# Expert retrieval in blocks: the query projection cut by heads and placed among the gathers, routes read from PSUM

## The chip, the cores and the metric

One core of a Trainium2 chip runs the whole kernel. The metric is the device time of one execution in microseconds, the median of three runs.
## The reference

One layer of a hybrid decoder, for a prompt of 512 tokens and eight samples of eight tokens (576 tokens in all, width 1024). The first half mixes tokens (an mLSTM branch and dilated window attention, merged by gates and projected); it also returns the caches rolled on by eight tokens. The second half, with which the change deals, is a product-key expert retrieval:

```
def _peer(h, wq, k1, k2, u, v):                       # h: (576, 1024), 8 heads, top 16
    q = (hb @ wq).reshape(blk, P_HEADS, P_QDIM)       # 8 heads x 256
    s1 = jnp.einsum('thd,nd->thn', q[..., :P_HALF], k1)
    s2 = jnp.einsum('thd,nd->thn', q[..., P_HALF:], k2)
    v1, i1 = lax.top_k(s1, P_TOPK)
    v2, i2 = lax.top_k(s2, P_TOPK)
    cand = v1[..., :, None] + v2[..., None, :]        # 16 x 16 candidates per head
    sc, pos = lax.top_k(cand, P_TOPK)
    eidx = take(i1 * P_NKEYS + i2, pos)               # 16 of 16384 experts
    g = jax.nn.softmax(sc, axis=-1)
    act = jax.nn.gelu(einsum('td,thkd->thk', hb, u[eidx]))
    return einsum('thk,thkd->td', g * act, v[eidx])
```

The result is normalised, scaled by a modulation row and added to the residual. Each token and head fetches 16 rows of u and v, 8 KB together.

## The kernel before

Tokens lie in five tiles: tiles 0 to 3 are the prompt (128 tokens each), tile 4 holds the 64 sample tokens. The program is a row of blocks with a barrier between them, each engine with its own instruction stream in the order in which the code is written; semaphores tie the streams together. Copies of the caches from memory to memory ("rolls", 88 pieces of up to 1 MB, `roll_pieces`) are issued by POOL beside the stages: one per unit of a projection (L399), two per step of the prompt attention (L599), one per unit of the merge gates (L731). SyncE waits for all of them at the very end (L1606).

`output_projection` (L1394) produces x1, h2 (tokens on partitions) and, by transposes, h2T (channels on partitions); beside it SyncE loads the first two of four 2 MB query weights. `query_projections` (L1509, through `project`, L372) multiplies all of h2T by all query weights: 16 units of 128 features, each of 8 matmuls of 288 columns for either half of the tokens, taken by ScalarE into qT. During it neither VectorE nor the gathers run.

`peer` (L1543) is the expert stage. Its unit is a slot n: one expert of one head for the 128 tokens of a tile. For each tile and head there is a *route* on VectorE (L1721 to L1759): two top-16 searches over 128 scores, 256 candidates, a top 16 of them, expert indices and softmax weights. ScalarE copies the scores of a whole tile out of PSUM first (`scores_taken`, L1665). For each slot POOL issues an indirect DMA of 128 rows of 8 KB, 1 MB (L1622), into one of `RING` = 10 slots; VectorE takes the dot product with h2 (L1767); ScalarE forms gelu, coefficient and a diagonal matrix (L1690, L1694, L1698), two slots at a time (`BATCH`); TensorE adds diagonal times v row in PSUM by two matmuls, four records (L1652), and so frees the slot, for which POOL waits:

```
if n >= RING:
    pool.wait_ge(s_v, n - RING + 1)
```

The order is tile by tile, head by head: 8 heads of tiles 0 to 3, and for tile 4 four pairs of heads packed into 128 partitions (POOL's copy, L1612), 36 blocks of 16 slots, 576 slots. `routed_beside` and `routed_at` (L1520, L1529) place the routes: beside tile 0 two per head (its own next one and tile 1's), beside tiles 1 and 2 one, beside tile 3 one for half of the heads, beside tile 4 none. At a tile's start TensorE computes the scores of the next tile (16 products, L1633), and at slot 4 the tile before is finished: ScalarE squares, VectorE mean, ScalarE root, VectorE scale and residual (`finish`).

## Time and profile before

| what | value |
|---|---|
| median of three runs | 2789.01 us (2787.6 to 2793.09) |
| profiled execution, its own time | 2792.53 us |
| its span, first to last instruction | 2790.7 us |
| mean granted TensorE clock | 0.904 |
| busy: PE, DVE, ACT, POOL | 2255.7, 1245.6, 703.4, 689.0 us |
| bytes moved by DMA | 850.42 MB, 691.32 of them on POOL's queue |

The profile is one execution, as the hardware recorded it. A group of instructions stands under its line in the code, with what it writes and reads, its count and its mean duration; behind it stands how long the engine had been idle just before and who ended that wait. Busy time of TensorE counts overlapping records once. "DMA share" is the mean busy share of the sixteen DMA engines; values up to 1.02 occur by rounding of the records. Idle time of an engine costs nothing where another sets the pace.

### The profile page before, as it was taken

How to read it: one execution, taken by the hardware profiler on the slowest of the kernel's cores; microseconds unless marked ns; L12 is line 12 of the kernel's file. 1: busy time of each engine (PE TensorE's matmuls, PEld its weight loads, DVE VectorE, ACT ScalarE, POOL GpSimd, SP SyncE). 2: the span in 40 equal slices, each digit the busy share in tenths (PEclk: the TensorE clock that was granted, in tenths of full speed). 3: DMA queues.
4: the chain of work that ended last, by engine and by line, in shares of the span. 5: the costliest groups of instructions: out<-in, count | busy, mean ns of one | idle time of the engine just before them, and what ended most of it. 6: DMA issues, size and time to landing. Idle time of an engine off the chain costs nothing.

```text
span 2790.7 us, 25027 instructions
## 1 busy us (share of the span) xinstructions
PE 2255.7 (81%) x9058; PEld 1285.6 (46%) x9058; DVE 1245.6 (45%) x3220; ACT 703.4 (25%) x2110; POOL 689.0 (25%) x682
## 2 busy tenths in 40 slices
PE   7999989966699978896777778777777877777776
PEld 2777458855478854475333333323332332332221
DVE  1000001211044422203899866776677677654544
ACT  2100012310023111101343333333333333322222
POOL 0000000000010000001443444444444444444342
PEclk8999989977789889998898898899888988999999
DMA  7666446879552025012999999999999999999997
GB/s 283 235 270 266 169 165 226 300 321 365 213 210 75 26 91 188 8 61 108 405 419 418 413 417 394 420 419 417 398 421 419 420 418 400 420 420 420 421 419 310
DMA packets 128002, 850.42 MB, mean 305 GB/s; under 512 B 14865, under 2 KB 24369, under 8 KB 46589
## 3 DMA queue, kind: packets, MB, share of 16 engines
q0 software_dynamic: 85760, 691.32, 60.8%
q1 hardware_dynamic: 40828, 154.95, 14.7%
q10 hardware_dynamic: 1290, 2.55, 0.3%
q8 instruction: 71, 1.16, 0.2%
q14 instruction: 53, 0.43, 0.0%
HBM read 836.43 MB, written 99.37 MB: 335 GB/s over the span
## 4 chain that ended last, share of the span: by engine, by line
DMA 20%; DVE 15%; PE 13%; ACT 2%; issue 2%; POOL 1%; ACTq 0%; POOLq 0%
DMA pr_ring<-in_uv,pr_idx 20%; PE ps L1652 12%; DVE pr_ring L1767 5%; POOL pr_ring L1622 1%; DVE pr_hot L1750 1%; DVE pr_hot L1746 1%; ACT pr_coef L1694 1%; DVE pr_ind L1725 1%; DVE pr_ind L1722 1%; DVE pr_pick L1753 1%; DVE pr_val L1724 1%; DVE pr_rest L1723 1%; DVE pr_val L1721 1%; DVE pr_pos L1725 1%; ACT pr_diag L1698 1%
## 5 line engine op out<-in xcount | busy, mean ns | idle before, releaser
L1652 PE MATMUL ps<-pr_ring,pr_diag 128*128 128x512 f32 (+1 forms) x2304 | 1097.8, 634 | 373.3 <-ACT pr_diag L1698 373.1
L1652 PEld LDWEIGHTS ps<-pr_ring,pr_diag 128*128 128x128 f32 (+1 forms) x2304 | 443.6, 198 | 1024.6 <-issue 517.2
L1767 DVE CUSTOM_DVE_ANT_0 pr_ring<-pr_ring,h 128x1024 f32<-128x1024 f32 x576 | 688.7, 1224 | 398.3 <-DMA pr_ring<-in_uv,pr_idx 396.9
L1622 POOL DMA_INDIRECT pr_ring<-in_uv,pr_idx x576 | 634.5, 1102 | 833.6 <-PE ps L1652 784.5
L1690 ACT ACTIVATE pr_gel<-pr_dots 128x2 f32<-128x2 f32 x288 | 58.6, 204 | 814.5 <-DVE pr_dots L1767 814.5
L1698 ACT ACTIVATE pr_diag<-ident,pr_coef 128x128 f32<-128x128 f32 x512 | 173.5, 386 | 0.0
L399 POOL DMA_DIRECT2D out_win_s<-in_cache x40 | 19.7, 492 | 569.4 <-PE ps L431 468.7
L1694 ACT ACTIVATE pr_coef<-pr_gel,pr_wgt 128x1 f32<-128x1 f32 x576 | 138.6, 287 | 27.1 <-ACT pr_gel L1690 0.4
L714 PE MATMUL ps<-trunk,gate_ring 128*128 128x288 f32 x512 | 130.3, 416 | 0.0
L430 PE MATMUL ps<-trunk,ap_ring 128*128 128x288 f32 x384 | 126.5, 411 | 2.9 <-PEq L323 2.9
L431 PE MATMUL ps<-trunk,ap_ring 128*128 128x288 f32 x384 | 125.7, 410 | 0.0
L1273 PE MATMUL ps<-sa_ring,sa_spread 128*32 128x128 f32 x1664 | 78.7, 371 | 51.3 <-DMA sa_ring<-in_cache 25.2
L299 DVE TENSOR_TENSOR late_rows<-ps,late_bias 128x512 f32<-128x512 f32 x2 | 1.4, 692 | 252.8 <-PE ps L289 252.8
L714 PEld LDWEIGHTS ps<-trunk,gate_ring 128*128 128x128 f32 x512 | 99.0, 195 | 27.2 <-ACT gate L722 0.3
L434 PE MATMUL ps<-ap_ring,trunk 128*128 128x512 f32 (+1 forms) x240 | 104.5, 595 | 0.0
L643 DVE CUSTOM_DVE_ANT_0 pa_prob<-ps,pa_masks 128x256 f32<-128x256 f32 (+3 forms) x48 | 19.4, 455 | 186.4 <-PE ps L608 186.4
L1273 PEld LDWEIGHTS ps<-sa_ring,sa_spread 128*32 128x32 f32 x1664 | 70.9, 152 | 60.0 <-issue 59.0
L1721 DVE MAX8 pr_val<-pr_sc 128x8 f32<-128x128 f32 x72 | 21.1, 293 | 152.5 <-ACT pr_sc L1665 151.2
L430 PE MATMUL ps<-h2T,qp_ring 128*128 128x288 f32 x256 | 84.3, 411 | 1.1 <-PEq L1412 1.1
L430 PEld LDWEIGHTS ps<-trunk,ap_ring 128*128 128x128 f32 x384 | 73.3, 192 | 23.8 <-issue 4.2
L431 PE MATMUL ps<-h2T,qp_ring 128*128 128x288 f32 x256 | 83.7, 409 | 0.0
L431 PEld LDWEIGHTS ps<-trunk,ap_ring 128*128 128x128 f32 x384 | 73.7, 192 | 20.4
(297 smaller groups left out, 2170.7 us busy)
## 6 DMA issues: line engine op xcount, KB each, us to landing
out_win_s<-in_cache POOLq DMA_DIRECT2D x64, 1020.0 KB, 7.1
late_ring<-in_w_ada SPq DMA_DIRECT2D x8, 2048.0 KB, 17.7
sa_ring<-in_kcacheB SPq DMA_DIRECT2D x8, 2048.0 KB, 12.8
sa_ring<-in_cache SPq DMA_DIRECT2D x8, 2048.0 KB, 13.8
out_win_s<-in_cache POOLq DMA_DIRECT2D x16, 1008.0 KB, 6.0
ap_ring<-in_w_attn_qk SPq DMA_DIRECT2D x6, 2048.0 KB, 11.2
sa_ring<-in_kcacheA SPq DMA_DIRECT2D x8, 1280.0 KB, 13.8
pr_ring<-in_uv,pr_idx POOLq DMA_INDIRECT x576, 14.6
```

The source lines that it names most:

```text
L430: pe.matmul(ps[:, u % 2, 0:TH], wc, rhsT[:, c, 0:TH], **on)
L431: mm = pe.matmul(ps[:, 2 + u % 2, 0:TH], wc, rhsT[:, c, TH:T], **on)
L434: mm = pe.matmul(ps[0:r, u % 2, :], rhsT[:, c, tile_cols(j)], w[:, c, :], **on)
L714: mm = pe.matmul(self.k.ps[:, self.BANK + half, 0:TH], self.ring[:, u % self.AHEAD, c, :], self.k.hT[:, c, half * TH:(half + 1) * TH], sta ...
L1273: mm = pe.matmul(o, operand(n // 2, s, w), ring[:, n % SR, (u * H + h) * P:(u * H + h + 1) * P], start=False, stop=last, skip_group_check= ...
L1622: pool.indirect_dma_start(ring[:, n % RING, :], None, d["uv"], bass.IndirectOffsetOnAxis(ap=idx[:, i % 2, q:q + 1], axis=0)).then_inc(arri ...
L1652: mm = pe.matmul(ps[0:r, 4 + 2 * (i % 2) + half, :], diag[:, n % RING, 0:r], ring[:, n % RING, o:o + CHUNK], start=q == 0, stop=q == last)
L1690: act.activation(gel[:, o:o + BATCH], dots[:, o:o + BATCH], ACT.Gelu).then_inc(s_gel, 1)
L1694: act.activation(coef[:, o + b:o + b + 1], gel[:, o + b:o + b + 1], ACT.Copy, scale=wgt[:, i % 2, q + b:q + b + 1]).then_inc(s_cf, 1)
L1698: act.activation(diag[:, o + b, 0:r], k.ident[:] if i < PT else k.fold[:], ACT.Copy, scale=coef[:, o + b:o + b + 1]).then_inc(s_dg, 1)
L1725: return dve.max_index(index[0:r, 8:16], out[0:r, 8:16], rest_)
L1767: ins = dve.tensor_tensor_reduce(u, u, e.h2[:, i, :], 1.0, 0.0, ALU.mult, ALU.add, dots[:, n % RING:n % RING + 1])
```

## The change

The block of the query projections is gone. Its work is cut into 32 pieces of 8 matmuls: for each head two halves of 128 features for the 384 tokens of tiles 0 to 2 (pieces 0 and 1) and two for the 192 tokens of tiles 3 and 4 (pieces 2 and 3). Head 0's pieces stand at the start of `peer`; those of head h + 1 stand in the blocks of head h (`query_pieces`): pieces 0 and 1 behind the first and the fifth pair of slots of tile 0's block, piece 2 behind the fifth pair of tile 1's, piece 3 behind the first of tile 2's. ScalarE takes each two pairs later. There is one PSUM bank for queries, one for scores and six for the sums of three tiles.

The slots now go head by head through tiles 0 to 2 (24 blocks), then through tile 3 and tile 4 (12 blocks). Scores are computed for one block, two blocks ahead; VectorE searches them where they lie in PSUM, and the copies to SBUF and POOL's packing are dropped. A route stands in every block ahead of its seventh pair of slots, for the block two further on. Finishing a tile is spread over four steps. Query weights are loaded per head, 1 MB in rows of 1 KB, two ahead of the stage and six within it. h2T lies in the half of `trunk` that the output projection does not read. The prompt attention issues three rolls per step.

```diff
                 for s in range(N):
                     pool.wait_ge(s_t, s + 1)
-                    for _ in range(min(2, len(k.rolls))):
+                    for _ in range(min(3, len(k.rolls))):
...
-                for n in range(e.wq.slots):
-                    sp.dma_start(e.wq.w[:, n], d["peer_wq"][n]).then_inc(e.wq.ready[n], 16)
-                e.wq.loaded = e.wq.slots
+                for h in range(QUERY_SLOTS):
+                    load_query_weights(sp, d, e, h)
...
+GROUP = 3
+GROUPED = GROUP * P
+BLOCKS = [(i, h) for h in range(PH) for i in range(GROUP)] + [(i, h) for i in range(GROUP, NCH) for h in range(heads_of(i))]
+FINAL = {i: b for b, (i, _) in enumerate(BLOCKS)}
+QUERY_SLOTS = 2
+QUERY_BANK, SCORE_BANK, SUM_BANK = 0, 1, 2
+def query_pieces(i, h, q):
+    return [piece for piece, at in enumerate(((0, 0), (0, 4), (1, 4), (2, 0))) if at == (i, q) and h + 1 < PH]
+def load_query_weights(sp, d, e, h):
+    o = h % 2 * 2 * P
+    sp.dma_start(e.wq[:, h % QUERY_SLOTS], d["peer_wq"][h // 2][:, :, o:o + 2 * P]).then_inc(e.wq_ready[h % QUERY_SLOTS], 16)
 RING = 10
-FINISH = 4
 BATCH = 2
+PER = TOPK // BATCH
+ROUTE, SCORE = 6, 2
+SQUARE, MEAN, ROOT, FINISH = 2, 3, 4, 5
...
+        def query_of(i, f):
+            if i < GROUP:
+                return first[:, f % 4, tile_cols(i)]
+            o = (i - GROUP) * P
+            return e.later[:, f, o:o + tile_rows(i)]
...
+                for h in range(QUERY_SLOTS, PH):
+                    sp.wait_ge(s_q, 4 * (h - QUERY_SLOTS + 1))
+                    load_query_weights(sp, d, e, h)
...
+                for b in range(len(BLOCKS)):
+                    pool.wait_ge(s_idx, b + 1)
+                    for j in range(TOPK):
+                        n = b * TOPK + j
                         if n >= RING:
                             pool.wait_ge(s_v, n - RING + 1)
                         pool.indirect_dma_start(ring[:, n % RING, :], None, d["uv"],
-                                                bass.IndirectOffsetOnAxis(ap=idx[:, i % 2, q:q + 1], axis=0)
+                                                bass.IndirectOffsetOnAxis(ap=idx[:, b % 4, j:j + 1], axis=0)
...
+                def query(h, piece):
+                    group, half = divmod(piece, 2)
+                    cols = slice(GROUPED, T) if group else slice(0, GROUPED)
+                    if piece == 0:
+                        pe.wait_ge(e.wq_ready[h % QUERY_SLOTS], 16 * (h // QUERY_SLOTS + 1))
+                    pe.wait_ge(s_qt, 4 * h + piece)
+                    for c in range(KD):
+                        mm = pe.matmul(ps[:, QUERY_BANK, 0:cols.stop - cols.start],
+                                       e.wq[:, h % QUERY_SLOTS, c, half * P:(half + 1) * P], e.h2T[:, c, cols],
+                                       start=c == 0, stop=c == KD - 1)
+                    mm.then_inc(s_q, 1)
+                def scores(b):
+                    i, h = BLOCKS[b]
+                    r = tile_rows(i)
+                    pe.wait_ge(s_qt, 4 * h + (2 if i < GROUP else 4))
+                    if b >= 1:
+                        pe.wait_ge(s_idx, b)
+                    for half in range(2):
+                        for o, head in ((0, h),) if i < PT else ((0, h), (TS, h + PH // 2)):
+                            mm = pe.matmul(ps[o:o + r, SCORE_BANK, half * P:(half + 1) * P], query_of(i, 2 * head + half),
+                                           keysT[:, half, :], start=True, stop=True)
                     mm.then_inc(s_sc, 1)
+                query(0, 0)
+                query(0, 1)
                 pe.wait_ge(s_keys, 16)
                 scores(0)
...
+                scores(1)
+                query(0, 2)
+                query(0, 3)
+                for b, (i, h) in enumerate(BLOCKS):
+                    r, bank = tile_rows(i), SUM_BANK + 2 * (i % GROUP)
+                    if i >= GROUP and h == 0:
+                        pe.wait_ge(s_ft, i - GROUP + 1)
+                    for q in range(PER):
+                        for j in range(q * BATCH, (q + 1) * BATCH):
+                            n = b * TOPK + j
+                            pe.wait_ge(s_dg, n + 1)
+                            for half in range(2):
+                                o = D + half * CHUNK
+                                mm = pe.matmul(ps[0:r, bank + half, :], diag[:, n % RING, 0:r],
+                                               ring[:, n % RING, o:o + CHUNK], start=h == 0 and j == 0,
+                                               stop=b == FINAL[i] and j == TOPK - 1)
+                            mm.then_inc(s_v, 1)
+                        if q == SCORE and b + 2 < len(BLOCKS):
+                            scores(b + 2)
+                        for piece in query_pieces(i, h, q):
+                            query(h + 1, piece)
...
+                def query_taken(h, piece):
+                    group, half = divmod(piece, 2)
+                    f = 2 * h + half
+                    act.wait_ge(s_q, 4 * h + piece + 1)
+                    if group == 0:
+                        ins = act.activation(first[:, f % 4, :], ps[:, QUERY_BANK, 0:GROUPED], ACT.Copy)
+                    else:
+                        ins = act.activation(e.later[:, f, :], ps[:, QUERY_BANK, 0:T - GROUPED], ACT.Copy)
+                    ins.then_inc(s_qt, 1)
...
+                query_taken(0, 0)
+                query_taken(0, 1)
+                route_exp(0)
+                query_taken(0, 2)
+                query_taken(0, 3)
+                for b, (i, h) in enumerate(BLOCKS):
+                    for q in range(PER):
+                        if b == 0 and q == 1:
+                            route_exp(1)
+                        if q == ROUTE and b + 2 < len(BLOCKS):
+                            route_exp(b + 2)
+                        if b >= 1 and FINAL[BLOCKS[b - 1][0]] == b - 1:
+                            if q == SQUARE:
+                                square(BLOCKS[b - 1][0])
+                            if q == ROOT:
+                                root(BLOCKS[b - 1][0])
+                        for piece in query_pieces(i, h, q - 2):
+                            query_taken(h + 1, piece)
+                        diags(b, q)
+                square(NCH - 1)
+                root(NCH - 1)
...
+                def route(b):
+                    dve.wait_ge(s_sc, b + 1)
+                    if b >= 4:
+                        dve.wait_ge(s_v, (b - 3) * TOPK)
                     for half in range(2):
-                        chain.step(top16(r, sc[:, i % 2, 2 * h + half, :], rest[:], val[:, half, :], ind[:, half, :]))
+                        chain.step(top16(ps[:, SCORE_BANK, half * P:(half + 1) * P], rest[:], val[:, half, :], ind[:, half, :]))
...
+                route(0)
                 dve.wait_ge(s_in, 16 * (2 + NS))
-                for i in order:
-                    for h in range(heads_of(i)):
-                        for q in range(h * TOPK, (h + 1) * TOPK, BATCH):
-                            if i and q == FINISH:
-                                finish(i - 1)
-                            for t, g in routed_at(i, q):
-                                route(t, g)
-                            dots_of(i, q)
+                for b in range(len(BLOCKS)):
+                    for q in range(PER):
+                        if b == 0 and q == 1:
+                            route(1)
+                        if q == ROUTE and b + 2 < len(BLOCKS):
+                            route(b + 2)
+                        if b >= 1 and FINAL[BLOCKS[b - 1][0]] == b - 1:
+                            if q == MEAN:
+                                mean(BLOCKS[b - 1][0])
+                            if q == FINISH:
+                                finish(BLOCKS[b - 1][0])
+                        dots_of(b, q)
+                mean(NCH - 1)
...
-        e.x1, e.h2, e.qT = sb("x1", [P, NCH, D]), sb("h2", [P, NCH, D]), trunk
-        with ExitStack() as mid:
-            e.h2T = sb("h2T", [P, KD, T], F32, mid)
-            e.wq = weight_ring(nc, k, "qp", mid, 2)
-            output_projection(nc, k, d, e)
-            query_projections(nc, k, d, e)
+        e.x1, e.h2, e.h2T = sb("x1", [P, NCH, D]), sb("h2", [P, NCH, D]), trunk[:, KD:, :]
+        e.wq = sb("pr_wq", [P, QUERY_SLOTS, KD, 2 * P])
+        e.wq_ready = [k.sem(f"pr_wq_ready{r}") for r in range(QUERY_SLOTS)]
+        free = trunk[:, 0:KD, :].rearrange("p c t -> p (c t)")
+        e.first = free[:, 0:4 * GROUPED].rearrange("p (f t) -> p f t", f=4)
+        e.later = free[:, 4 * GROUPED:].rearrange("p (f t) -> p f t", f=2 * PH)
+        output_projection(nc, k, d, e)
```

TensorE's stream from the last query matmuls into the expert stage, before the change (qp_ring and pr_wq are the query weights, trunk holds queries or h2T, pr_keysT the keys, pr_ring the gathered rows; a matmul counts once here):

```order
L431 MATMUL ps<-h2T,qp_ring 128x288
L391 UNCONDITIONAL_BRANCH
L1626 UNCONDITIONAL_BRANCH
L1633 MATMUL ps<-pr_keysT,trunk 128x128 x32
L1652 MATMUL ps<-pr_ring,pr_diag 128x512 x256
L1633 MATMUL ps<-pr_keysT,trunk 128x128 x16
L1652 MATMUL ps<-pr_ring,pr_diag 128x512 x256
```

The same place with the change:

```order
L1619 UNCONDITIONAL_BRANCH
L1629 MATMUL ps<-trunk,pr_wq 128x384 x16
L1642 MATMUL ps<-pr_keysT,trunk 128x128 x4
L1629 MATMUL ps<-trunk,pr_wq 128x192 x16
L1663 MATMUL ps<-pr_ring,pr_diag 128x512 x4
L1629 MATMUL ps<-trunk,pr_wq 128x384 x8
L1663 MATMUL ps<-pr_ring,pr_diag 128x512 x8
L1642 MATMUL ps<-pr_keysT,trunk 128x128 x2
L1663 MATMUL ps<-pr_ring,pr_diag 128x512 x8
L1629 MATMUL ps<-trunk,pr_wq 128x384 x8
L1663 MATMUL ps<-pr_ring,pr_diag 128x512 x24
```

Of 256 query matmuls (the first row stands for the last of them) 16, of 384 columns, are left ahead of the first scores; 16 of 192 columns follow, and the next head's stand between the sums.

POOL's stream in the prompt attention:

```order
 L599 DMA out_win_s<-in_cache 16x16320 x25
-L599 DMA out_win_s<-in_cache 16x16128 x7
+L599 DMA out_win_s<-in_cache 16x16128 x16
+L599 DMA out_win_s<-in_cache 16x7680 x7
 L584 UNCONDITIONAL_BRANCH
```

Sixteen rolls more are issued there, 7 of them half-size.

## Rows read from the trace of the kernel before

**Rows 1.** The page, in 40 slices of the span: GB/s moved by DMA.
```profile
GB/s 283 235 270 266 169 165 226 300 321 365 213 210 75 26 91 188 8 61 108 405 419 418 413 417 394 420 419 417 398 421 419 420 418 400 420 420 420 421 419 310
```
**Rows 2.** Busy us by stretch: PE, PEld, DVE, ACT, POOL, PEclk, DMA share, GB/s.
```profile
1161.00:1288.00 127.00, 125.90 (x512) 98.40 (x512) 0.00 (x0) 11.27 (x33) 0.49 (x1) 0.99 0.10 37
1288.00:1308.00 20.00, 9.28 (x64) 8.92 (x64) 9.35 (x39) 3.88 (x8) 1.24 (x3) 0.83 0.19 59
1400.00:1600.00 200.00, 156.45 (x311) 66.20 (x310) 179.77 (x520) 78.74 (x239) 83.65 (x78) 0.86 1.01 417
1700.00:1960.00 260.00, 191.41 (x405) 80.44 (x404) 184.45 (x469) 84.38 (x278) 113.89 (x102) 0.88 1.01 419
2480.00:2740.00 260.00, 190.93 (x414) 65.11 (x415) 129.72 (x212) 66.66 (x264) 103.70 (x104) 0.99 1.01 420
```
**Rows 3.** Timeline, 1160 to 1308 us: start, duration, instruction, [idle before, releaser].
```profile
1160.41 0.60 ACT L1476 ACTIVATE h2T<-ps 128x512 f32<-128x512 f32 x1 [3.96 <-PE ps L1448]
1161.49 1.30 PE L430 MATMUL ps<-h2T,qp_ring 128*128 128x288 f32 x2 [1.11 <-PEq L1412]
...
1290.33 5.47 PE L1633 MATMUL ps<-pr_keysT,trunk 128*128 128x128 f32 x32 [2.94 <-DMA pr_keysT<-in_keysT]
...
1297.93 0.30 DVE L1721 MAX8 pr_val<-pr_sc 128x8 f32<-128x128 f32 x1 [138.72 <-ACT pr_sc L1665]
...
1307.41 0.23 DVE L1759 TENSOR_SCALAR pr_wgt<-pr_ex,pr_rex 128x16 f32<-128x16 f32 x1
...
1307.93 1.02 POOL L1622 DMA_INDIRECT pr_ring<-in_uv,pr_idx  x1 [18.35 <-DVE pr_wgt L1759]
```
**Rows 4.** The chain of waits, last two of its transfers: start, us until landed.
```profile
2731.74 18.66 DMA pr_ring<-in_uv,pr_idx
2756.68 18.64 DMA pr_ring<-in_uv,pr_idx
```
**Rows 5.** Tile pr_ring, issue to landing: all 576 gathers, then those of 1400:1640.
```profile
DMA to landing us min/median/max: 5.7/14.6/19.9
...
DMA to landing us min/median/max: 8.6/12.1/19.2
```
**Rows 6.** Tile h2T: ns min/median/max, first and last start in us.
```profile
L431 PE MATMUL ps<-h2T,qp_ring x256: 405/407/688, 1162.6 to 1287.0; 128*128 128x288 f32 x128
```
**Rows 7.** DMA queues in 391:516 (rolls on q0, mp_ring on q1): packets, MB, share.
```profile
q0 software_dynamic: 656, 21.94, 47.9%
q1 hardware_dynamic: 5200, 5.24, 13.3%
```
**Rows 8.** Timeline of PE: a run of 512-column records; the first behind a route.
```profile
1104.72 13.90 PE L1438 MATMUL ps<-op_w,trunk 128*128 128x512 f32 x32
...
1388.70 0.70 PE L1652 MATMUL ps<-pr_ring,pr_diag 128*128 128x512 f32 x1 [3.56 <-ACT pr_diag L1698]
```
**Rows 9.** Groups of DVE: one operand in PSUM, then all in SBUF.
```profile
L1117 DVE TENSOR_TENSOR ml_hn<-ml_iw,ps 128x512 f32<-128x512 f32 (+1 forms) x5 | 3.4, 683 | 0.3 <-ACT ml_iw L1070 0.3
L1120 DVE TENSOR_TENSOR ml_hn<-ml_hn,ml_rd 128x512 f32<-128x512 f32 (+1 forms) x5 | 3.4, 689 | 0.2
```
**Rows 10.** Busy us by stretch, the end of tile 0 (columns of Rows 2).
```profile
1670.00:1690.00 20.00, 11.75 (x22) 5.16 (x23) 17.15 (x38) 8.02 (x28) 4.49 (x5) 0.67 0.85 342
```
**Rows 11.** Prompt attention's end and sample attention: stretches, POOL's last rolls.
```profile
520.00:550.00 30.00, 30.00 (x163) 24.36 (x162) 8.77 (x30) 16.44 (x26) 2.89 (x6) 1.00 0.99 379
550.00:583.00 33.00, 27.27 (x160) 22.88 (x158) 3.01 (x10) 9.65 (x19) 1.93 (x4) 0.97 0.53 189
583.00:660.00 77.00, 45.22 (x896) 38.92 (x896) 10.26 (x32) 1.28 (x1) 0.00 (x0) 0.68 0.99 408
...
571.53 0.96 POOL L599 DMA_DIRECT2D out_win_s<-in_cache  x2 [9.27 <-PE ps L622]
```
**Rows 12.** Timeline of the output projection's first tile.
```profile
1095.87 0.16 DVE L1487 TENSOR_TENSOR op_ss<-op_ss 128x1 f32<-128x1 f32 x1 [33.26 <-DMA op_rows<-rows]
...
1103.79 1.09 PE L1448 MATMUL ps<-ident,h 128*128 128x128 f32 x8 [2.72 <-DVE h L1506]
```

204 lines of the change are left out of this document (63 added, 141 removed).

## The prediction, made before the run

> **What bounds the kernel now.** I read the page's slices first, then the busy time by stretch, then the chain of waits and the transfers' landing times. The slices show one stage that fills half the program [rows 1]: from slice 20 on the DMA engines are full and move about 420 GB/s, while the three slices before the ramp (1116 to 1325 us) move 8, 61 and 108 GB/s. The stretches name both sides [rows 2]. From 1161 to 1288 us the query projections keep TensorE busy for 125.90 of 127 us while the DMA share is 0.10; from 1288 to 1308 us scores and the first route run, at 0.19. Then the gathers run: DMA share 1.01 wherever one looks, VectorE at 90%, 71% or 50% busy, TensorE at 74 to 78%. So the expert stage is bound by bytes: 576 gathers of 1.05 MB. The first is issued at 1307.93 [rows 3], the last at 2756.68 [rows 4], 575 intervals in 1448.8 us, 2.52 us each. Where no route is computed the chain repeats every ten gathers in 24.94 us [rows 4], 2.49 each, the pure price of the bytes.
>
> Two things follow. The time before the first gather is wholly on the path and holds little DMA work; and work put beside the gathers is free as long as the ring of ten slots never empties. The landing times measure that reserve: the first gather, alone, lands 5.7 us after its issue; with two routes per sixteen gathers (tile 0) the shortest is 8.6, the median 12.1 [rows 5], still at share 1.01. At its tightest the ring has 8.6 - 5.7 = 2.9 us to spare.
>
> **The change, part by part.** All sums are against the profiled run: span 2790.7, its own time 2792.5. The median of the runs is 2789.0, 3.5 below, and the sum is carried over to it.
>
> *Start of the gathers.* Of the stretch from 1161.49 to 1307.93 (146.4 us) only two query pieces, one pair of score products and one route stay ahead of the first gather. The projection rows [rows 6] put a 288-column record at (1287.0 - 1162.6) / 255 / 2 = 0.244 us, so 384 columns are 0.325 and a piece of 8 matmuls (16 records) 5.2 us. The query bank is single, so the second piece waits for ScalarE's copy: about 0.9 us, estimated from 0.60 for a 512-wide copy [rows 3] and two handovers, once for each piece. The first records run at the lower clock (1.30 us for two [rows 3]): 1 us. Scores are 4 records of some 0.17 (32 take 5.47 [rows 3]), 0.7 with the drain. The route takes 9.7 us (1297.93 to 1307.64) and POOL issues 0.3 later [rows 3]. Sum 1 + 5.2 + 0.9 + 5.2 + 0.9 + 0.7 + 0.2 + 10.0 = 24.1, plus 0.9 of allowance for further handovers: first gather at 1186.5, **-121.4**. If both pieces ran wholly at the lower clock it would be -111; without the allowance -122.3. The copies of scores by ScalarE and POOL's packing lie in the same stretch and go with it. Group 1's first two pieces stand behind the first gather, in time that TensorE spends waiting for dots.
>
> *Weights beside the gathers.* Six of the eight 1 MB head weights now load in a stage that is full. Their rows are 1 KB runs, like the loads of mp_ring, which stand alone on q1 in [rows 7]: 5.24 MB in 5200 packets for 13.3% of 125 us = 16.6 us of all engines. Six loads are 6.29 MB: **+19.9**. At the gathers' own 420 GB/s it would be 15.0, the lower bound; twice the measured price, 40, is the upper, should two queues disturb each other. The Trainium skill (DMA: Bandwidth & Descriptors, Specifications) gives 512 B as the smallest transfer at line rate; by it these loads would cost the 15.0. The row of 1 KB packets gives 315 GB/s and so disagrees, and I go by the row.
>
> *Query pieces on TensorE.* In tile 0 TensorE is busy 156.45 of 200 us [rows 2], 31.3 per 40 us block of sixteen gathers, against 27.8 (64 records at 13.90 / 32 = 0.434 [rows 8]) at full clock; the rest is the slower clock after each route, behind which it stands idle 3.56 us [rows 8]. A block of tile 0 gets two pieces of 5.2 us: 41.7 against the 39.9 that its bytes take. Blocks of tiles 1 and 2 get one 192-column piece of 2.6 us and stay at 34. So seven blocks are over by 1.8 us, 13 us in all if the ring carries nothing; the next block has 6 us in hand to recover. The first piece stands six gathers behind the end of a route; by then TensorE, at 1.74 us a gather, has gained 6 x (2.49 - 1.74) = 4.5 us on the DMA, with the 2.9 of reserve 7.4, above 5.2. I take **+4** (0 to 13). ScalarE copies a piece before the pair two steps on, with TensorE still holding one pair (3.5 us) against the copy and the pair's own 1.7 us: no stall. Each block now has one route where tile 0 had two; VectorE has time (184.45 busy of 260 with one [rows 2]).
>
> *Route from PSUM.* The same instructions read the score bank. An add out of PSUM took 683 ns, the same form out of SBUF 689 [rows 9]: nothing. Maxima are not shown from PSUM; at 0.1 us more for each of the 6 reads, or less, a route changes by 0.6 us, under VectorE's 11 us of slack per block: 0. Were VectorE full, it would be 36 x 0.6 = 22.
>
> *Tile ends.* Where a tile ends, sixteen score products, the copy, the finish and routes come together, and the DMA runs short: in the worst of four such windows 342 GB/s [rows 10] against 420, 3.7 us; the others are 2.3 to 3.3, some 12 us in all. Scores come by the block now and the finish is split over four steps, but VectorE still waits for the last product of the finished tile. Half goes: **-6** (0 to -12).
>
> *Rolls.* Sixteen cache copies leave the later stages for the prompt attention, three per step; seven are half-size, and these come last. From 520 to 550 us that stage is already at share 0.99 [rows 11]; the three extra copies there take 3 x 2.7 us of all engines (rolls cost 47.9% x 125 / 21.94 = 2.7 us a megabyte [rows 7]), a backlog of 8 us. Behind it there is room (share 0.53 to 583), and the last two steps, one of them at 571.53, now carry 1.5 MB in place of 2. So nothing should reach the sample attention, which is at 0.99 from 583 on [rows 11] and would feel it: **0** (0 to 3). The stages they leave are TensorE's: 0.
>
> *Output projection.* VectorE starts on op_rows at 1095.87 and TensorE then waits 2.72 us for it [rows 12]; the weight loads queued behind are halved: **-1** (0 to -2.7).
>
> Sum: -121.4 + 19.9 + 4 + 0 - 6 + 0 - 1 = -104.5; the span becomes 2686.2, the run's own time 2688.0, and from the median 2789.0 - 104.5 = **2684.5 us**. The tail behind the last gather keeps its form.
>
> **The rivals.** (a) *The ring runs dry at the pieces.* For it: 41.7 against 39.9, and ScalarE is now tied to TensorE at four points per head. Against: the reserve of 7.4 us. If every block of tile 0 loses between its whole excess and one piece, 7 x 1.8 = 13 to 7 x 5.2 = 36 us in place of the 4: 2693 to 2717. (b) *The loads are dear.* Weights at 40 instead of 19.9, rolls at 3: 2708. (c) *The other side: no piece is hidden.* If at each of the 28 pieces the DMA stood still for the piece's length, 7 x (2 x 5.2 + 2 x 2.6) = 109 us come back in place of the 4; with the boundary gain gone too, 2684.5 + 105 + 6 = 2795, slower. It decides from (104.5 - 6 + 4) / 28 = 3.7 us lost per piece. Against it is the 1.01 share with landings down to 8.6 us [rows 2, 5]. It would come about if TensorE's granted clock, 0.86 with two routes per block and 0.99 with none [rows 2], stayed near the lower level (1.2 GHz) while pieces are added; but the clock is lowest here where TensorE idles behind routes [rows 8], and those become fewer in tile 0, so I give the case little. The Trainium skill (TensorE: Matmul & The Clock Gate, Part 1) says that activity releases the clock and idling withdraws it; by that rule the pieces would raise the granted clock, and the time would stay that of the forecast. (d) *The start does not move* because something else holds the first gather. The weights of head 0 are issued in the stage before, and keys and gates land while the pieces run; I see nothing.
>
> **How the numbers follow.** Forecast 0.75 (its own range 2668 to 2704: from -4.9 for the weights, -4, -6 and -1.7 below to 9 for the pieces, 6 for the tile ends, 3 and 1 above); (a) 0.12; (b) 0.07; (c) 0.05; (d) 0.01. The range runs from 2668 to 2720, into (a) and (b). Within 0.2% (5.6 us, about what a measurement of this kernel can tell from no change) needs a near cancellation: 0.01. Faster 0.94, slower 0.05.
>
> **What would show it.** The first gather at about 1186 us and the last about 1469 us behind it: (1448.8 + 19.9 + 4 - 6). DMA share 1.00 or more in the blocks of tiles 0 to 2; the shortest landing there not under 6 us; TensorE near 90% busy in tile 0's blocks. A gather interval above 2.58 us in the first 24 blocks with DMA share under 0.97 would show (a); full share with fewer gathers per us, (b). A sample attention that starts or ends late would show the rolls. The prediction is wrong if the first gather is later than 1200, or if VectorE's reads of PSUM lengthen a route beyond 11 us.

## The result, and the profile after

| | before | after |
|---|---|---|
| median of the runs, us | 2788.31 (2787.44 to 2793.09, 4 runs) | 2682.59 (2675.73 to 2688.66, 4 runs) |
| ratio | | 0.9617, 95% interval 0.959 to 0.9643 |
| profiled run, its own time and span | 2792.53, 2790.7 | 2688.66, 2686.9 |
| first gather, last gather | 1307.93, 2756.68 | 1186.09, 2652.93 |
| between the two | 1448.75 | 1466.84 |

The change takes 105.7 us off the median; 104.5 were forecast. From profile to profile it is 2792.53 - 2688.66 = 103.9. The runs of after lie 12.9 us apart, so an agreement to 1 us is closer than the forecast could be by its own working, and is in part luck. The profiled run of after is the slowest of its four, so terms of a few us are read inside the expert stage and not from these times.

The page of after: busy times, the slices, and the two large DMA queues.

```profile
PE 2238.8 (83%) x9074; PEld 1277.5 (48%) x9074; DVE 1248.4 (46%) x3220; ACT 695.9 (26%) x2094; POOL 702.0 (26%) x680
...
PEclk8999989986798969979899998999898898998889
DMA  6666648989821021339999999999999999999997
GB/s 271 227 256 262 224 169 291 336 339 384 320 84 68 20 95 72 93 140 418 416 418 413 416 416 406 417 411 419 406 420 412 416 420 411 416 411 410 413 420 303
...
q0 software_dynamic: 85760, 691.32, 63.5%
q1 hardware_dynamic: 48572, 154.95, 15.4%
```

Against [rows 1] the full slices begin at 1209 us instead of 1325 (the nineteenth slice of 67.2 us, the twentieth of 69.8), and they read 406 to 420 GB/s throughout.

The timeline of after, from the end of the output projection to the first gather (start, duration, instruction, [idle before, releaser]):

```profile
1160.29 8.37 PE L1629 MATMUL ps<-trunk,pr_wq 128*128 128x384 f32 x16 [1.26 <-PEq L1412]
...
1169.23 5.43 PE L1629 MATMUL ps<-trunk,pr_wq 128*128 128x384 f32 x16 [0.58 <-ACT trunk L1681]
...
1175.33 0.68 PE L1642 MATMUL ps<-pr_keysT,trunk 128*128 128x128 f32 x4 [0.67 <-ACT trunk L1681]
1176.05 0.30 DVE L1750 MAX8 pr_val<-ps 128x8 f32<-128x128 f32 x1 [18.19 <-PE ps L1642]
...
1185.57 0.23 DVE L1785 TENSOR_SCALAR pr_wgt<-pr_ex,pr_rex 128x16 f32<-128x16 f32 x1
...
1186.09 1.07 POOL L1615 DMA_INDIRECT pr_ring<-in_uv,pr_idx  x1 [354.78 <-DVE pr_wgt L1785]
```

From the first query product to the first gather it is 25.8 us where [rows 3] has 146.4: two pieces, two copies, one pair of scores, one route. The first piece takes 8.37 us and the same work right behind it 5.43; the granted clock of the stretch is 0.76, the first row below. The other three rows are the expert stage in stretches, with the columns of [rows 2].

```profile
1160.00:1186.00 26.00, 14.53 (x37) 7.96 (x37) 9.09 (x38) 2.66 (x5) 0.00 (x0) 0.76 0.14 45
1200.00:1860.00 660.00, 562.43 (x1422) 269.38 (x1421) 454.93 (x1135) 215.00 (x716) 287.37 (x252) 0.92 1.01 415
1860.00:2160.00 300.00, 246.40 (x603) 114.90 (x604) 210.54 (x515) 104.75 (x349) 137.59 (x120) 0.91 1.01 414
2160.00:2640.00 480.00, 363.00 (x817) 143.37 (x816) 334.30 (x811) 160.16 (x531) 208.60 (x190) 0.89 1.01 415
```

The DMA share is full in all three stretches of the stage, and TensorE has room: 562.43 of 660 us in the busiest. The stage is bound by bytes as before, starts 121.8 us earlier and lasts 18.1 longer. Below are the times from a gather's issue to its landing, of all 576 and then of those issued in 1200 to 1850. The shortest are close to those of [rows 5], the median of all is the same, and that of the busy blocks is 14.2 where tile 0 had 12.1 before.

```profile
DMA to landing us min/median/max: 5.5/14.6/21.5
```
```profile
DMA to landing us min/median/max: 8.6/14.2/21.4
```

### The profile page after: what moved, and what is told of

It reads as the page before. It is cut to its first block, busy times and chain, and to the rows that moved or that the text cites. A ratio compares the mean times of both kernels' runs of the same rounds, so it can differ in the third digit from the quotient of the medians.

```text
span 2686.9 us, 25099 instructions
## 1 busy us (share of the span) xinstructions
PE 2238.8 (83%) x9074; PEld 1277.5 (48%) x9074; DVE 1248.4 (46%) x3220; ACT 695.9 (26%) x2094; POOL 702.0 (26%) x680
## 4 chain that ended last, share of the span: by engine, by line
DMA 18%; DVE 17%; PE 16%; issue 2%; ACT 2%; POOL 1%; ACTq 0%; POOLq 0%
DMA pr_ring<-in_uv,pr_idx 18%; PE ps L1663 16%; DVE pr_ring L1793 4%; POOL pr_ring L1615 1%; DVE pr_hot L1773 1%; DVE pr_hot L1777 1%; DVE pr_ind L1754 1%; DVE pr_ind L1751 1%; DVE pr_pick L1780 1%; ACT pr_coef L1715 1%; DVE pr_val L1753 1%; DVE pr_rest L1752 1%; DVE pr_val L1750 1%; DVE pr_pos L1754 1%; DVE pr_pos L1751 1%
## 5 line engine op out<-in xcount | busy, mean ns | idle before, releaser
L1615 POOL DMA_INDIRECT pr_ring<-in_uv,pr_idx x576 | 649.1, 1127 | 1173.5 <-PE ps L1663 782.9
L1629 PE MATMUL ps<-trunk,pr_wq 128*128 128x192 f32 (+1 forms) x512 | 134.3, 417 | 2.3 <-PEq L1412 1.3
L1629 PEld LDWEIGHTS ps<-trunk,pr_wq 128*128 128x128 f32 x512 | 93.9, 196 | 48.1 <-issue 17.8
L434 PE MATMUL ps<-ap_ring,trunk 128*128 128x512 f32 (+1 forms) x240 | 104.5, 595 | 0.0
L1437 PE MATMUL ps<-op_w,trunk 128*128 128x512 f32 (+1 forms) x160 | 71.8, 609 | 10.7 <-DMA op_w<-in_w_out 10.7
## 6 DMA issues: line engine op xcount, KB each, us to landing
late_ring<-in_w_ada SPq DMA_DIRECT2D x8, 2048.0 KB, 17.5
pr_ring<-in_uv,pr_idx POOLq DMA_INDIRECT x576, 14.6
```

Source lines behind the costliest of these rows:

```text
L434: mm = pe.matmul(ps[0:r, u % 2, :], rhsT[:, c, tile_cols(j)], w[:, c, :], **on)
L1437: mm = pe.matmul(ps[0:r, 2 * (i % 2) + n, :], k.hT[:, c, tile_cols(i)], w[:, n, c, :], start=c == 0, stop=c == KD - 1)
L1615: pool.indirect_dma_start(ring[:, n % RING, :], None, d["uv"], bass.IndirectOffsetOnAxis(ap=idx[:, b % 4, j:j + 1], axis=0)).then_inc(arri ...
L1629: mm = pe.matmul(ps[:, QUERY_BANK, 0:cols.stop - cols.start], e.wq[:, h % QUERY_SLOTS, c, half * P:(half + 1) * P], e.h2T[:, c, cols], sta ...
```

## The experiments

Each edit is made in the changed kernel. "Stage" is the time from the first to the last gather, "start" that from the first query product to the first gather, both from the profile. The measure for what a profile can tell of the stage: after has 1466.84, and `rolls_two`, whose stage is the same code, 1464.55. So a difference under some 2.4 us is none; three further kernels whose edits barely touch the stage, `first_tile_first`, `scores_copied` and `finish_together`, lie between 1464.46 and 1465.66. The start is 24.3 to 25.9 us in the nine profiles that have this code.

**Query pieces ahead of the stage.**

```diff
-                    for c in range(KD):
+                    for c in range(KD if h == 0 else 1):
...
+                for h in range(1, PH):
+                    for w in (GROUPED, GROUPED, T - GROUPED, T - GROUPED):
+                        for c in range(KD):
+                            pe.matmul(ps[:, QUERY_BANK, 0:w], e.wq[:, 0, c, 0:P], e.h2T[:, c, 0:w], ...)
                 pe.wait_ge(s_keys, 16)
                 scores(0)
```

> The seven later heads' query pieces inside the expert stage shrink to one product of eight each, and TensorE does the same amount of products (112 of 384 columns, 112 of 192) before the first scores; the queries of heads 1 to 7 are therefore partial sums. Theory (the start of the gathers is on the path one for one, pieces beside them are nearly free): first gather later by 14 x 5.2 + 14 x 2.6 = 109 us, at about 1295; first to last gather 1463 to 1467; time about 2682.6 + 109 - 4 = 2788. Rival (work ahead of the stage is partly regained inside it, because something else sets the stage's length): less than 90 us longer. Rival (pieces beside the gathers cost their own length): first to last gather shrinks by 60 to 100 us and the time stays near 2700.

Measured: 2790.47 us (2787.37 to 2795.06, 10 runs), ratio to before 1.0008 (0.9998 to 1.0018). The timeline:

```profile
1151.57 7.74 PE L1629 MATMUL ps<-trunk,pr_wq 128*128 128x384 f32 x16 [1.26 <-PEq L1412]
...
1159.89 5.43 PE L1629 MATMUL ps<-trunk,pr_wq 128*128 128x384 f32 x16 [0.58 <-ACT trunk L1687]
...
1165.89 108.91 PE L1652 MATMUL ps<-trunk,pr_wq 128*128 128x384 f32 x448 [0.58 <-ACT trunk L1687]
...
1285.31 1.07 POOL L1615 DMA_INDIRECT pr_ring<-in_uv,pr_idx  x1 [459.08 <-DVE pr_wgt L1791]
```

108.91 us of products stand ahead of the scores, and the time grows by 2790.47 - 2682.59 = 107.9. The stage is 1466.32 us. The time before the first gather counts one for one, within a few us, and this alone takes back the whole gain.

**Pieces inside the stage, shrunk to an eighth.** The first line of the diff above alone.

> Only the reduction of the pieces inside the stage (one product of eight; the queries of heads 1 to 7 are partial sums), nothing added ahead. It measures what the pieces cost where they are. Theory: 4 us less, between 0 and 13: 2679, first to last gather 1463. Rival (ring runs dry at the pieces): 13 to 36 less. Rival (pieces are not hidden): about 95 less.

Measured: 2679.31 us (2676.7 to 2683.75), 0.961 (0.9594 to 0.9626). The stage is 1466.0 us, no shorter than the changed kernel's beyond what profiles differ by. So seven eighths of the twenty-eight pieces' work cost nothing that shows beside the gathers; the rivals of 13 to 36 and of 95 us fall.

**Pieces inside the stage, issued twice.**

```diff
-                    for c in range(KD):
+                    for c in list(range(KD)) * (1 if h == 0 else 2):
```

> Every product of the pieces inside the stage for heads 1 to 7 is issued twice (the queries come out doubled). A tile-0 block of TensorE goes from 41.7 to 52.1 us, blocks of tiles 1 and 2 from 34 to about 37, against 39.9 of bytes: a group of three blocks is 126 against 120. Theory (only what goes over the bytes' time is paid, and it is recovered little): tile-0 blocks lengthen by some 7 to 12 us each, 50 to 85 us in all, time 2735 to 2765. Rival (the ring and the roomy blocks behind carry most of it): under 30 us, below 2712. Rival (every added us is paid): 109 us, 2790.

(The second round starts its sum anew, so the queries are computed twice and not doubled.) Measured: 2719.32 us (2714.34 to 2720.79), 0.975 (0.9734 to 0.9766): 36.7 us over the changed kernel, below the theory's 50 to 85 and above the rival's 30. The stage is 1498.12 us, 31.3 longer. Stretches of the length of three blocks, one each of tiles 0, 1 and 2 (a group): the changed kernel, the same with light pieces, and the same with double ones. In the first and the last the stretch begins within 2 us of a block of tile 0, in the light one 11 us behind it.

```profile
1303.00:1429.00 126.00, 106.82 (x271) 50.95 (x270) 86.30 (x212) 40.75 (x137) 54.51 (x48) 0.92 1.01 415
```
```profile
1303.00:1429.00 126.00, 95.48 (x212) 41.59 (x212) 87.10 (x217) 41.52 (x137) 53.92 (x48) 0.87 1.01 418
```
```profile
1303.00:1349.00 46.00, 41.79 (x106) 20.07 (x105) 31.28 (x81) 13.37 (x45) 18.43 (x18) 0.96 1.00 408
1349.00:1384.00 35.00, 35.00 (x93) 17.18 (x93) 20.70 (x43) 10.51 (x39) 14.06 (x14) 1.00 0.91 370
...
1303.00:1429.00 126.00, 117.91 (x332) 61.15 (x331) 82.67 (x198) 37.53 (x130) 51.78 (x48) 0.97 0.98 401
```

Here is the limit that the prediction's rival (a) describes: with TensorE busy for all of 35 us the DMA share falls to 0.91 and 370 GB/s. The change itself stays short of it over this group, at 1.01 and 415 GB/s, against 418 with light pieces. The second thing to see is the granted clock: 0.87 with light pieces, 0.92 with the change's, 0.97 with double ones. In these three kernels it rises with the work.

**No weight loads in the stage.**

```diff
-                for h in range(QUERY_SLOTS, PH):
-                    sp.wait_ge(s_q, 4 * (h - QUERY_SLOTS + 1))
-                    load_query_weights(sp, d, e, h)
...
-                        pe.wait_ge(e.wq_ready[h % QUERY_SLOTS], 16 * (h // QUERY_SLOTS + 1))
+                        pe.wait_ge(e.wq_ready[h % QUERY_SLOTS], 16)
```

> The six head weights are not loaded inside the stage; heads 2 to 7 multiply by the weights of heads 0 and 1 again (their queries are those heads'). Theory: six loads cost 3.1 us of all transfer engines each, so the first to last gather shrinks by 19 us and the time is 2664. Rival (the loads cost the gathers' own price per byte): 15 less, 2668. Rival (two queues disturb each other): 25 to 40 less. Rival (transfers are not what bounds the stage in the blocks with pieces): under 10 less.

Measured: 2666.25 us (2663.06 to 2668.61), 0.9554 (0.9538 to 0.957). The stage is 1447.74 us, 19.1 shorter than after and 16.8 shorter than that of `rolls_two`; the time is 16.3 shorter. These lie between the theory's 19 and the 15 of the rival (the gathers' own price per byte) and do not part the two; the next run does. The rivals of 25 to 40 and of under 10 fall. Without the loads the stage is as long as before the change (1448.75): within the 2.4 us that profiles differ by, they are the whole of the 18.1 us by which it grew.

**Weights in long rows.**

```diff
-    sp.dma_start(e.wq[:, h % QUERY_SLOTS], d["peer_wq"][h // 2][:, :, o:o + 2 * P])...
+    sp.dma_start(e.wq[:, h % QUERY_SLOTS], d["peer_wq"][h])...
...
-        "peer_wq": chunks(a["peer_wq"][0]),
+        "peer_wq": np.stack([by_row(a["peer_wq"][0][:, o:o + 2 * P]) for o in range(0, PH * 2 * P, 2 * P)]),
```

> The same 1 MB head weights, but laid out so that each partition's part of one head is a single run of 8 KB and not eight runs of 1 KB. Theory (1 KB runs move at 315 GB/s of all engines, 8 KB runs at 420): six loads cost 15.0 instead of 18.7 to 19.9, so 4 to 5 us less, about 2678; the queue's transfer time in the stage falls from 3.1 to 2.5 us a load. Rival (the run length does not matter): no difference, q1's time unchanged.

Measured: 2678.43 us (2672.98 to 2681.42), 0.9598 (0.9585 to 0.9611), stage 1460.85. DMA queues and issues in 1200 to 1800 us (packets, MB, share of 16 engines), of the changed kernel and then of this one:

```profile
q1 hardware_dynamic: 5341, 5.39, 2.6%
...
pr_wq<-in_peer_wq SPq DMA_DIRECT2D x5, 1024.0 KB, 26.6
```
```profile
q1 hardware_dynamic: 773, 5.55, 2.2%
...
pr_wq<-in_peer_wq SPq DMA_DIRECT2D x5, 1024.0 KB, 9.2
```

2.6% of 600 us for 5.39 MB are 2.89 us a megabyte; 2.2% for 5.55 MB are 2.38. On 6.29 MB that is 18.2 against 15.0, 3.2 us less; the stage shrank by 6.0 against after and 3.7 against `rolls_two`, the time by 4.2. The intervals of the two times overlap, so it is the queue's own rows that settle it (the shares are rounded to 0.1, which leaves each price open by some 0.05). A load also lands in 9.2 us instead of 26.6.

**Tile 0's columns first.**

```diff
+                def first_tile():
+                    pe.wait_ge(e.wq_ready[0], 16)
+                    for half in range(2):
+                        for c in range(KD):
+                            mm = pe.matmul(ps[:, 6 + half, 0:P], e.wq[:, 0, c, half * P:(half + 1) * P],
+                                           e.h2T[:, c, 0:P], start=c == 0, stop=c == KD - 1)
+                    mm.then_inc(s_f1, 1)
...
-                query(0, 0)
-                query(0, 1)
+                first_tile()
                 pe.wait_ge(s_keys, 16)
                 scores(0)
+                query(0, 0)
+                query(0, 1)
```

> Ahead of the first gather only tile 0's 128 columns of head 0 are projected (into the sum banks of tile 2, one copy), the other columns of tiles 1 and 2 follow behind the first scores. Theory (the path to the first gather counts one for one): 32 records of about 0.11 to 0.2 us and one copy in place of two pieces of 8.4 and 5.4 and two copies, first gather at 1177 to 1179 in place of 1186.1, time 7 to 9 us less, about 2675. Rival (the stage's first gathers then wait for scores of tile 1 that come too late): first gather earlier, but the second block's gathers later, no gain.

Measured: 2672.52 us (2670.05 to 2675.51), 0.9585 (0.9572 to 0.9598), 10.1 less than the changed kernel. Its timeline:

```profile
1151.28 5.89 PE L1626 MATMUL ps<-trunk,pr_wq 128*128 128x128 f32 x32 [1.11 <-PEq L1412]
...
1157.20 0.38 ACT L1736 ACTIVATE trunk<-ps 128x256 f32<-128x256 f32 x1 [6.40 <-PE ps L1626]
1157.73 0.68 PE L1653 MATMUL ps<-pr_keysT,trunk 128*128 128x128 f32 x4 [0.56 <-ACT trunk L1736]
...
1168.95 1.07 POOL L1616 DMA_INDIRECT pr_ring<-in_uv,pr_idx  x1 [343.38 <-DVE pr_wgt L1800]
```

The start falls from 25.8 to 17.7 us and the stage stays (1465.26). The pieces that follow cover the other 256 columns. Again one for one as far as it can be read: 8 us of the 10 are in the start, and the other 2 are within what the stages before it vary by (below).

**Fewer copies in the prompt attention.**

```diff
-                    for _ in range(min(3, len(k.rolls))):
+                    for _ in range(min(3 if s == 0 else 2, len(k.rolls))):
```

> Two cache copies per step of the prompt attention as before the change (three in its first step, since one place behind is gone); fifteen copies go back beside the convolution, gates and mLSTM. Theory: no difference (0 to 3 us), sample attention starts within 1 us of before. Rival (the change's 1.4 us of earlier sample attention came of the copies): sample attention later by 1.4. Rival (the copies held something up): 3 us and more less.

Measured: 2683.21 us (2682.11 to 2683.77), 0.9621 (0.9607 to 0.9636). Sample attention starts at 581.75, in after at 581.76, and at 583.32 before the change. In the eleven other profiles it starts between 581.4 and 583.6, `pieces_double` last, so the start before the change is inside the spread. The moved copies cost and gained nothing that shows.

**Scores copied to SBUF.**

```diff
+                def copy_scores(b):
+                    act.wait_ge(s_sc, b + 1)
+                    act.activation(score[:], ps[:, SCORE_BANK, 0:2 * NKEYS], ACT.Copy).then_inc(s_cp, 1)
...
-                    dve.wait_ge(s_sc, b + 1)
+                    dve.wait_ge(s_cp, b + 1)
```

> ScalarE copies the scores of each block to SBUF and VectorE's maxima read the copy, as before the change, in the new block order. Theory: reading the scores from PSUM costs VectorE nothing, the copy of 256 columns stands only in front of the first gather: plus 0.5 to 1 us in all, time the same; a route is as long as before. Rival (maxima are slower from PSUM): a route shortens by over 0.5 us and the stage with it. Rival (ScalarE is tight): the stage gets longer by 5 us and more.

Measured: 2681.98 us (2678.74 to 2683.06), 0.9614 (0.9599 to 0.9629); stage 1464.46. VectorE's groups of the changed kernel, reading PSUM, and of this one, reading the copy:

```profile
L1750 DVE MAX8 pr_val<-ps 128x8 f32<-128x128 f32 x72 | 21.4, 297 | 19.4 <-PE ps L1642 18.2
...
L1751 DVE FIND_INDEX8 pr_ind<-pr_val,ps 128x8 uint32<-128x128 f32 x72 | 20.9, 291 | 0.0
```
```profile
L1760 DVE MAX8 pr_val<-pr_score 128x8 f32<-128x128 f32 x72 | 21.1, 292 | 19.9 <-ACT pr_score L1694 18.6
L1761 DVE FIND_INDEX8 pr_ind<-pr_val,pr_score 128x8 uint32<-128x128 f32 x72 | 20.5, 285 | 0.0
```

Out of PSUM the two take 5 and 6 ns longer, hundredths of a microsecond in a route of 9.8. Leaving the copy out gains nothing that shows in the stage; ahead of the first gather it is 0.4 us (start 26.2 for 25.8).

**The tile's finish in one step.**

```diff
-SQUARE, MEAN, ROOT, FINISH = 2, 3, 4, 5
+SQUARE, MEAN, ROOT, FINISH = 2, 2, 2, 2
```

> Square, mean, root and finish of a tile stand at one step (the third pair of the next block) again, instead of in four steps. Theory (part of the 6 us forecast for the tile ends comes from spreading them): 3 to 6 us longer over the four tile ends inside the stage, mostly in blocks 22 to 24 and 32. Rival (they come by the new order and the scores by the block alone): under 1.5 us.

Measured: 2682.07 us (2676.63 to 2683.75), 0.9613 (0.9595 to 0.9632); stage 1465.66. The blocks behind a tile end do lengthen, 43.2, 44.9 and 44.3 us for blocks 22, 24 and 32 instead of 40.4, 41.6 and 40.3, and later ones are short by as much (25: 36.8 for 41.5, 33: 37.3 for 41.0): blocks 22 to 27 together take 245.9 us for 246.1. The late issues are paid back by the ring within a few blocks; they are no lost transfers here. The theory falls: spreading the finish gains nothing.

**Late routes left out.**

```diff
                     dve.wait_ge(s_sc, b + 1)
+                    if b >= 28:
+                        dve.sem_inc(s_nt, 1)
+                        dve.wait_ge(s_ex, b + 1)
+                        dve.sem_inc(s_idx, 1)
+                        return
```

> The last eight blocks' routes (blocks 28 to 35, in tiles 3 and 4) are left out: VectorE only hands the semaphores on, so these blocks gather the rows of earlier indices. In the profile of the changed kernel blocks 28 to 33 (sixteen gathers each) take 40.3 to 41.3 us, in the one of before the blocks without a route 39.9. Theory (a route in one piece of 9.8 us holds VectorE long enough for the transfers to run short for a moment, 0.5 to 1 us a block): blocks 26 to 33 fall to 39.9 to 40.4, the last gather 4 to 8 us earlier, time about 2677. Rival (the routes are free, the difference comes of something else): under 2 us.

Measured: 2677.0 us (2675.04 to 2689.01), 0.9613 (0.9587 to 0.9639). The time cannot tell 4 us here; the profile can. The stretch 2440 to 2600 us, in the changed kernel and in this one:

```profile
2440.00:2600.00 160.00, 120.64 (x281) 44.24 (x280) 114.25 (x283) 54.15 (x181) 67.58 (x63) 0.87 1.01 414
```
```profile
2440.00:2600.00 160.00, 117.87 (x279) 39.37 (x280) 80.24 (x133) 53.98 (x182) 70.85 (x64) 1.00 1.01 420
```

Blocks 26 to 33, beside which the eight routes stood, take 322.7 us instead of 326.6. That is 0.5 us a route, the lower end of the theory, but after is the slowest of its kind here: in the seven other profiles whose VectorE code of these blocks is unchanged they take 324.6 to 326.3 us, and from block 26 to the last gather the kernel without late routes is 1.7 to 2.6 us shorter than they, 3.2 shorter than after. So the eight routes cost some 2 to 4 us together. (The rows gathered without routes are repeats of earlier ones; the 420 GB/s of the stretch are those of [rows 2] for fresh rows, so this is not what made it faster.) Where it goes is seen in the 40 slices of 2400 to 2500 us (2.5 us each) of the changed kernel, where routes run from 2418 to 2428 and from 2459 to 2469, and in POOL's row behind the second:

```profile
GB/s 393 423 419 419 426 429 423 419 423 419 419 419 419 419 413 383 347 390 429 426 419 429 419 423 423 419 413 419 419 423 419 347 397 367 406 426 426 423 426 426
```

```profile
2476.74 1.33 POOL L1615 DMA_INDIRECT pr_ring<-in_uv,pr_idx  x1 [11.22 <-PE ps L1663]
```

Behind a route no slot comes free; POOL issues nothing for 11.22 us, and as it resumes the transfers fall to 347 GB/s for a few us, at 2438 to 2445 and at 2477 to 2487. The DMA share does not show it: it stays at 1.01. Summed over such slices against 420 GB/s (an estimate from rounded rates), 2400 to 2600 us lack 2.8 us of transfers in after, 2.5 in `rolls_two`, 1.3 in `scores_copied` and 0.1 without the routes.

**Routes in three pieces.**

```diff
-                        if q == ROUTE and b + 2 < len(BLOCKS):
-                            route(b + 2)
+                        if ROUTE - 2 <= q <= ROUTE and b + 2 < len(BLOCKS):
+                            (route_first, route_second, route_third)[q - ROUTE + 2](b + 2)
```

> Each route is cut into three pieces of 3.4, 3.0 and 3.4 us, with a pair of dot products between them; nothing is added or left out. Theory (what costs is the length in one piece for which VectorE leaves the ring alone): blocks of tiles 3 and 4 fall from 40.3 to 41.3 us to about 40, those with one piece of queries by as much, first to last gather 8 to 20 us less, time 2662 to 2675. Rival (the ring carries a whole route already, the 40.9 is the bytes' time): no difference. Rival (the first piece then waits for its scores): 5 us and more longer.

Measured: 2684.05 us (2678.91 to 2687.68), 0.9624 (0.9607 to 0.9641); stage 1463.74. The blocks become even (blocks 3 to 20: 39.0 to 44.7 us instead of 34.5 to 45.8) and the granted clock of 2440 to 2600 us is 0.96 instead of 0.87, but the rate there is 415 GB/s against 414. No gain that shows: the 8 to 20 us forecast for it are not there. The median time from issue to landing rises from 14.6 to 17.5 us, so more gathers are under way at once, and the bytes still take as long. What the routes cost by was not settled.

**Four parts together**: long rows, tile 0's columns first, a third slot for weights, split routes.

```diff
-QUERY_SLOTS = 2
+QUERY_SLOTS = 3
```

> Together: head weights in runs of 8 KB, tile 0's columns first, a third slot for head weights (five loads in the stage instead of six), routes in three pieces. If the parts add: 6 us for the rows, 8 for the first tile, 2.5 for the slot, 8 to 20 for the routes: first to last gather 1436 to 1450, 17 to 18 us from the first query product to the first gather, time 2646 to 2660. Rival (with the transfers nearly back to back the blocks with two pieces bound the stage by TensorE): little of the last two comes, 2665.

Measured: 2663.44 us (2662.76 to 2668.57), 0.956 (0.9544 to 0.9575), start 18.1 us, stage 1459.7. Rows (4.2) and first tile (10.1) as measured alone, and one load of 2.5 us less, make 2682.59 - 16.8 = 2665.8; the time is 2.4 below it, within the spread of the runs. The routes' 8 to 20 did not come, so the range of 2646 to 2660 was missed and the rival's 2665 is near. It beats the changed kernel by 0.7%, with intervals that do not touch (0.9544 to 0.9575, 0.959 to 0.9643).

## Why the prediction was right, step by step

| step | forecast | measured | read from |
|---|---|---|---|
| start of the gathers | -121.4 | -121.8 | 1307.93 to 1186.09; -120.6 inside the stretch, -1.2 from earlier stages (which vary by 12) |
| weights beside gathers | +19.9 | +16.8 to +19.1; +18.2 by the queue | `no_weight_loads`, queue rows |
| query pieces | +4 (0 to 13) | 0 (within 2.4) | `pieces_light` |
| route from PSUM | 0 | 0 | `scores_copied` |
| tile ends | -6 (0 to -12) | about -1 (within 2.4), with pieces and routes | stage without loads, 1447.74 for 1448.75 |
| rolls | 0 | 0 | `rolls_two` |
| output projection | -1 (0 to -2.7) | not to be told | below |
| sum | -104.5 | -103.9 (profiles), -105.7 (medians) | |

*Start of the gathers.* The step holds in size and in kind, and with it falls rival (d), that something else holds the first gather. `pieces_ahead` puts 108.9 us of products back and loses 107.9; `first_tile_first` takes 8 more away and gains them. The stretch is 25.8 us for a sum of 25.0. Inside it two entries were off and nearly cancel: the first piece took 8.37 us and not 1 + 5.2, at a granted clock of 0.76 for the stretch; the copies hold TensorE up for 0.58 and 0.67 and not 0.9, and the general allowance of 0.9 went unused. That the first gather stands at 1186.09 for a forecast 1186.5 is luck: with the same code ahead of it, it stands between 1175.0 and 1186.1 in nine profiles.

*Weights.* The 1 KB row of [rows 7] gave 3.17 us a megabyte, the loads themselves 2.89, rows of 8 KB 2.38. So the price of short runs is real, and taking the row over the gathers' own rate was right; it was 10% too dear. The upper bound, twice the price should two queues disturb each other, was not reached. The Trainium skill (DMA: Bandwidth & Descriptors, Specifications) has transfers of 512 B and more at line rate; the trace differs, with 2.89 against 2.38 for 1 KB against 8 KB.

*Pieces.* The mechanism was right and the size too large. The forecast let each of seven blocks exceed 39.9 us by 1.8 and took part of it as lost. Of every three blocks two run over (up to 45.8 us) and the one between them is short (34.5 to 37.8), so over three blocks TensorE's 106.82 of 126 us fits. By these lengths the unit in which the ring balances is the group of three blocks and not the block. `pieces_double` shows where that ends; its price, 31 to 37 us, was again overestimated, at 50 to 85.

*Tile ends.* This is the step that failed. The end of tile 0 in [rows 10] moved 342 GB/s; the stretches in which the finished tiles are taken out hold far more in after.

```profile
2110.00:2130.00 20.00, 20.00 (x50) 8.91 (x49) 12.60 (x23) 9.21 (x27) 13.37 (x12) 1.00 1.00 407
...
2150.00:2170.00 20.00, 18.82 (x47) 8.35 (x46) 10.76 (x20) 9.21 (x27) 13.05 (x11) 1.00 1.01 418
...
2190.00:2210.00 20.00, 19.59 (x49) 8.69 (x47) 10.92 (x21) 9.64 (x31) 12.77 (x11) 0.99 1.01 420
...
2510.00:2530.00 20.00, 17.24 (x34) 6.43 (x35) 12.75 (x25) 7.39 (x29) 9.55 (x8) 0.80 1.00 396
```

So the windows on which the 12 us rested are better, and yet the stage is no shorter. The whole shortfall shows why. At 2.494 us, the clean interval of [rows 4], 575 intervals are 1434.0 us; before, the stage lost 1448.75 - 1434.0 = 14.7 beyond that. After, with 18.2 for the loads, it loses 1466.84 - 1434.0 - 18.2 = 14.6. The loss left the tile ends and is spread in dips of a few us over the whole stage, at 414 to 415 GB/s where [rows 2] has 417 to 420: by slices of 2.5 us, each 200 us from 1200 to 2600 lack 1.3 to 3.7 us at 420 GB/s (an estimate from rounded rates). Eight late routes hold 2 to 4 us of it. A route alone is not the whole cause: [rows 2] has 417 and 419 GB/s in stretches with two and with one of them per block. Forecasting half of a window's loss as gain, without asking where the same routes would stand now, was the mistake; nothing in the sum priced a route beside the gathers. It shows little in the total since the +4 of the pieces was too large by nearly as much. Neither the finish in four steps (`finish_together`) nor the length of a route in one piece (`route_split`) sets it, and what causes the rest of the 14.6 stays open.

*Rolls, PSUM, output projection.* The first two came as forecast. For the third: from the first product of the output projection to the first query product it is 1161.49 - 1070.96 = 90.5 us before and 1160.29 - 1069.46 = 90.8 after. But with the code of after this stage takes 87.5 to 94.0 us in the other profiles, so a term of 1 us can neither be confirmed nor denied here.

*The rivals.* (a) is excluded for the change itself by `pieces_light` (the share of 1.01 alone would not do it, since it hides dips), and is real one doubling further. (b): the loads are at 18, not 40. (c): a lost 3.7 us per piece was needed; seven eighths of the work of 28 pieces cost within 2.4 us together. Its condition, a clock that stays low, is turned round: 0.87, 0.92, 0.97 with light, normal and double pieces. By the rule of the Trainium skill (TensorE: Matmul & The Clock Gate, Part 1) that activity releases the clock, this is the direction to expect, and the trace agrees.

*What was to be seen.* First gather 1186.09 for 1186; stage 1466.84 for 1466.7; share 1.01; shortest landing 8.6 for "not under 6"; TensorE at 85% over a group, where "near 90" was said of tile 0's blocks alone. The stage length matches to 0.2 us only because of the two errors named above; each step is good to a few us.

## What to carry to other kernels

When one stage is full of transfers and the one before it is empty of them, count the time to the first transfer: all of it is on the path, and only what the first transfer needs belongs in front of it. Then cut that again, as 128 of the 384 columns did here. Work put beside the transfers was free here as long as it fitted on its engine over the three blocks in which the ring balanced; loads put there cost their bytes, more in rows of 1 KB than of 8 KB. Do not book a dip in a window as a gain: sum the shortfall against the clean interval over the whole stage, since a loss can move without shrinking.

## What was not expected of the hardware

- The same code before the expert stage ends at different times from run to run. The first query product stands between 1149.3 and 1161.5 us in the fourteen profiles, while sample attention starts at 581.4 to 583.6 and the output projection at 1062.3 to 1071.0. Most of the spread arises between those two, the rest in the output projection. The stage itself repeats to some 2.4 us, its tail behind the last gather to 0.1 (33.9 to 34.0). With one profile a kernel, a few us are found inside a stage or not at all.
- The DMA share does not tell a dip: it reads 1.01 over stretches at 414, 415 and 420 GB/s. The rate in narrow slices does.
- Taking routes away raised TensorE's granted clock from 0.87 to 1.00 as adding pieces raised it from 0.87 to 0.97, but not by the same way. With pieces it waits less often: its waits on pr_diag between 1200 and 1800 us fell from 34 (134.6 us) with light pieces to 23 (87.5) with the change's and 11 (45.3) with double ones, some 4 us each. Without the late routes it waits about as long in all, but in shorter pieces: between 2440 and 2600 us 32 times (42.2 us) for 11 times (39.4) in after.
- The first query piece behind the output projection took 8.37, 7.74, 7.47 and 7.88 us in the profiles of after, `pieces_ahead`, `pieces_double` and `weights_long_rows`, and between 6.91 (`rolls_two`) and 8.41 (`route_split`) in all that have it; the same piece right behind it took 5.43. So the 1 us allowed for the slow start is 1.5 to 3.
